# Delta-rule stage of a decoder step: key blocks first, sample work re-placed among the heads' periods

## The reference

```python
decay = jnp.exp(jnp.where(tril, G[..., :, None] - G[..., None, :], -jnp.inf))
kb = k * beta[..., None]
A = jnp.where(tril & (eye == 0), jnp.einsum('bhncd,bhnsd->bhncs', kb, k) * decay, 0.0)
Tm = lax.linalg.triangular_solve(eye + A, jnp.broadcast_to(eye, A.shape), left_side=True, lower=True)
u = Tm @ (v * beta[..., None])
w = Tm @ (kb * jnp.exp(G)[..., None])
...
v_new = u_n - w_n @ S
o = qg_n @ S + qk_n @ v_new
S = S * gl_n[..., None, None] + jnp.swapaxes(kd_n, -1, -2) @ v_new
```

## Time and profile before

| | us |
|---|---|
| median of 3 timed runs | 2983.39 (2982.0 to 2985.71) |
| profiled execution, its own time | 2976.36 |
| its span in the trace | 2974.6 |
| delta-rule stage, barrier to barrier | 1072.3 to 1277.9 |
| TensorE, VectorE, ScalarE, GpSimd busy in the span | 2795.1, 2312.4, 1363.6, 316.1 |

### The profile page before, as it was taken

How to read it: one execution, slowest core, us unless ns; L and a number is a source line. 1 busy time by engine, 2 the same in 40 slices (tenths; PEclk the granted TensorE clock), 3 DMA queues, 4 the chain that set the end, 5 groups by cost and what they waited for, 6 DMA issues and landing times.

```text
span 2974.6 us, 55263 instructions
## 1 busy us (share of the span) xinstructions
PE 2795.1 (94%) x22589; PEld 2669.7 (90%) x22589; DVE 2312.4 (78%) x3566; ACT 1363.6 (46%) x2316; POOL 316.1 (11%) x303
## 2 busy tenths in 40 slices
PE   8999999989988968889889999999999999999995
PEld 8999999988877657789889999999999999999995
DVE  6656777877677778755688888888888888888898
ACT  5434455556545624521254444444444453434352
POOL 0010000024270212323300000000000000000010
PEclk9999999999999989999999999999999999999998
DMA  7564443458632864563343434444443465434333
GB/s 221 177 203 109 128 120 108 120 193 277 227 138 99 358 173 116 147 169 94 90 157 112 140 106 135 123 127 121 121 139 112 138 190 167 146 119 156 103 122 117
DMA packets 520849, 440.12 MB, mean 148 GB/s; under 512 B 36184, under 2 KB 476687, under 8 KB 513979
## 3 DMA queue, kind: packets, MB, share of 16 engines
q1 hardware_dynamic: 456278, 301.49, 35.3%
q0 software_dynamic: 20048, 82.12, 7.4%
q10 hardware_dynamic: 44272, 52.98, 5.3%
HBM read 378.31 MB, written 66.55 MB: 150 GB/s over the span
## 4 chain that ended last, share of the span: by engine, by line
PE 49%; DVE 6%; issue 1%; ACT 1%; DMA 0%; DVEq 0%; ACTq 0%
PE i L3219 42%; PE i L140 7%; DVE f_half L3709 1%; DVE x_blocks L3747 1%; PE i L3207 1%; DVE y_rows L3829 0%; DVE y_rows L3834 0%; DVE h_rows L3742 0%; DVE resid L3594 0%; DVE resid L3597 0%; DVE w_ring L3698 0%; DVE x_blocks L3615 0%; PE i L3228 0%; DMA x_blocks<-s_blk 0%; DVE ln_parts L3753 0%
## 5 line engine op out<-in xcount | busy, mean ns | idle before, releaser
L3219 PE MATMUL i<-x_blocks,f_half 128*128 128x272 f32 x10752 | 1361.1, 289 | 23.4 <-DVE h_rows L3742 11.1
L3219 PEld LDWEIGHTS i<-x_blocks,f_half 128*128 128x128 f32 x10752 | 1351.7, 189 | 28.5 <-DVE x_blocks L3747 12.2
L570 PE MATMUL a<-xb_in,w_half 128*128 128x272 f32 x4200 | 545.5, 291 | 8.2 <-DVE w_half L972 4.2
L570 PEld LDWEIGHTS a<-xb_in,w_half 128*128 128x128 f32 x4200 | 534.9, 189 | 17.2 <-issue 7.2
L3440 ACT CAST f_half<-w_ring 128x1024 fp32r<-128x1024 f32 (+2 forms) x370 | 346.3, 936 | 405.6 <-PE i L3219 351.1
L3709 DVE TENSOR_TENSOR f_half<-w_ring,f_half 128x1024 fp32r<-128x1024 f32 (+2 forms) x362 | 393.0, 1086 | 80.7 <-ACT f_half L3440 78.0
L3709 DVE TENSOR_TENSOR f_half<-f_sum,f_half 128x1024 fp32r<-128x1024 f32 (+2 forms) x148 | 159.4, 1077 | 82.0 <-ACT f_half L3440 82.0
L972 DVE TENSOR_TENSOR w_half<-w_ring,w_half 128x1024 fp32r<-128x1024 f32 x129 | 157.4, 1222 | 79.3 <-ACT w_half L708 78.9
L3440 ACT CAST f_half<-f_sum 128x1024 fp32r<-128x1024 f32 (+2 forms) x148 | 138.7, 937 | 149.7 <-PE i L3219 149.7
L708 ACT CAST w_half<-w_ring 128x1024 fp32r<-128x1024 f32 x125 | 131.3, 1050 | 109.7 <-PE a L570 106.0
L3192 POOL TENSOR_TENSOR f_half<-w_ring,f_half 128x512 fp32r<-128x512 f32 x8 | 13.8, 1731 | 1410.5 <-ACT f_half L3440 1410.5
(11 more groups left out here) (559 smaller groups left out, 4084.3 us busy)
## 6 DMA issues: line engine op xcount, KB each, us to landing
w_ring<-in_ffn_w_up_dram SPq DMA_DIRECT2D x88, 1024.0 KB, 6.0
w_ring<-in_w_in_dram SPq DMA_DIRECT2D x52, 1024.0 KB, 8.8
w_ring<-in_ffn_w_down_dram SPq DMA_DIRECT2D x24, 1536.0 KB, 7.0
w_ring<-in_w_o_dram SPq DMA_DIRECT2D x16, 1024.0 KB, 6.0
x_blocks<-s_blk ACTq DMA_DIRECT2D x17, 816.0 KB, 5.2
s_proj<-st ACTq DMA_DIRECT2D x48, 272.0 KB, 2.6
s_blk<-x_sums ACTq DMA_DIRECT2D x22, 544.0 KB, 6.7
kv_ring<-in_cmp_w_dram SPq DMA_DIRECT2D x16, 512.0 KB, 8.0
```

The costliest lines, as they stand in the source:

```text
L570: last = nc.tensor.matmul(ps[bank][:, 0:HT2], half(q, w)[:, k], XB[v[j]][:, k], start=j in (0, 1, 3) and k == 0 and i == 0, stop=k == HK - ...
L3219: last = nc.tensor.matmul(ps[bank][:, 0:HT2], half(e, j, wl_)[:, s], XB[:, x0 + s, xl_, BLK_OF[j]], start=start and s == 0 and i == 0, sto ...
```

## The change

Opening (period -1). TensorE makes all key blocks first, then head 0's rows, the sample keys, head 0's key products, and the rest. VectorE takes the blocks ahead of the samples' work, which is spread between block rows. ScalarE instead of VectorE scales the sample tiles (8 instructions a tile). The state products and what follows leave the period.

Half of `keys_decayed` now stands behind the third `state_step`, two instructions before the end, and only the second half signals aq_r. The diff, cut to its core:

```diff
 SyncE, rows_in(h)
-                        sp.wait_ge(kk_ps, h - 1)
+                        sp.wait_ge(kk_ps, 2 * (h - 1))
 GpSimd
+                def s_lows(src, dst, at, n):
+                    gp.wait_ge(s_hi, n)
+                    for m, q in enumerate(at):
+                        nc.gpsimd.tensor_tensor(dst[32 * q:32 * q + NS].rearrange("p h d -> p (h d)"), src.rearrange("p h d -> p (h d)"),
+                                                dst[0:NS].bitcast(F32).rearrange("p h d -> p (h d)"), ALU.subtract).then_inc(s_lo, 1)
+                        gp.wait_ge(s_lo, 2 * n - 1 + m)
+
+                def states_decayed(h):
+                    nc.gpsimd.tensor_tensor(SSA[:, h], SSA[:, h], GLS[:, :, h:h + 1].broadcast_to((P, B, HD)), ALU.mult).then_inc(sg, 1)
+
                 for i in PERIODS:
                     lev, new, old, _ = heads(i)
+                    if i == 1:
+                        gp.wait_ge(sg, 3)
+                        s_lows(VNS[:], VN4, (1, 3), 2)
                     if new is not None:
                         if new == 0:
                             gp.wait_ge(x_l, X_DONE + 1)
+                        else:
+                            gp.wait_ge(scaled_r, 2 * new + 1)
...
+                    if i == -1:
+                        gp.wait_ge(tt_i, 2)
+                        s_lows(KDS_F[:], KDS, (2, 3), 1)
+                    if i == 0:
+                        gp.wait_ge(wsp_s, GH // 2)
+                        gp.wait_ge(pre, 1)
                     if old is not None:
-                        gp.wait_ge(wsp_s, 1)
-                        gp.wait_ge(pre, 1)
-                        nc.gpsimd.tensor_tensor(SSA[:, old], SSA[:, old], GLS[:, :, old:old + 1].broadcast_to((P, B, HD)), ALU.mult).then_inc(sg, 1)
-                        gp.wait_ge(s_lo, 2)
...
+                    if 0 <= i <= 2:
+                        for h in range(3 * i, min(3 * i + 3, GH)):
+                            states_decayed(h)
 TensorE
-                def keys(h):
+                def keys(h, k):
                     r = h % 2
-                    pe.wait_ge(nat_r, h + 1)
-                    pe.wait_ge(scaled_r, 2 * h + 2)
-                    for t in range(QT):
+                    if k == 0:
+                        pe.wait_ge(nat_r, h + 1)
+                        pe.wait_ge(scaled_r, 2 * h + 2)
+                    for u in range(2):
+                        t = 2 * k + u
...
-                def s_states():
+                def s_states(h2):
...
                     if i == -1:
+                        key_blocks(0, GH).then_inc(kx_ps, 1)
+                        rows(0)
                         s_keys()
-                        key_blocks(0, 6)
                         s_turn()
-                        rows(0)
+                        keys(0, 0)
+                        keys(0, 1)
                         s_y()
-                        key_blocks(6, GH).then_inc(kx_ps, 1)
+                        s_values()
                         s_d()
-                        s_values()
-                        keys(0)
                         pe.wait_ge(inv_s, 1)
                         s_w()
-                        s_states()
                         continue
...
                     if done is not None:
                         step_s(done, 3)
+                        sample_s(done, 1)
                     if i == 0:
+                        s_states(0)
+                    if i == 1:
                         s_o()
                     if lev is not None:
                         products_d(lev, 4)
+                    if i == 0:
+                        s_states(2)
...
 ScalarE
+                def s_scaled(dst, c):
+                    for h in range(GH):
+                        last = nc.scalar.mul(dst[:, h], ps[6 + h // 4][0:NS, (h % 4) * HD:(h % 4 + 1) * HD], c[:, h:h + 1])
+                    return last
...
+                    if i == 1:
+                        act.wait_ge(vn_s, 1)
+                        s_highs(VNS[:], VN4, (0, 2))
...
-                    if i == 0:
-                        s_squares()
...
+                    if i == 1:
+                        s_squares()
 VectorE, opening
-                s_decay()
                 blocks_log()
+                s_decay()
                 scaled_keys(0)
-                s_keys()
                 decay(0)
-                dve.wait_ge(k_ps_s, 1)
-                s_scaled(((KGS, BE[0:NS, QC]), (KDS_F[:], ED[0:NS, QC]))).then_inc(k_r_s, 1)
-                s_turned()
+                blocks_weights()
                 scaled_queries(0)
-                blocks_weights()
                 blocks_keys()
...
-                dve.wait_ge(vp_s, 1)
-                s_rows(VNS, 0).then_inc(vn_s, 1)
 VectorE, one period
                     if new is not None:
                         scaled_keys(new)
+                    if done is not None:
+                        sample_states(done, 1)
                     if lev is not None:
                         place_d(lev, 4)
-                    if i == 0:
+                    if i == 1:
                         dve.wait_ge(op_s, 1)
                         s_rows(ONS, 1).then_inc(or_s, 1)
...
+                    if new is not None:
+                        keys_decayed(new, 0)
                     if old is not None:
                         state_step(old, 1)
+                        sample_states(old, 0)
                     if i == 0:
-                        s_lows(KDS_F[:], KDS, (2, 3), 1)
-                        s_lows(VNS[:], VN4, (1, 3), 2)
-                        s_normed()
-                    if new is not None:
-                        keys_decayed(new)
-                    if old is not None:
-                        sample_states(old, 0)
-                        v_copy(old, 2)
+                        keys_decayed(new, 1)
...
+                    if i == 2:
+                        s_normed()
                     if old is not None:
+                        v_copy(old, 2)
...
                         state_step(old, 2)
-                        sample_states(old, 1)
+                        if new is not None:
+                            keys_decayed(new, 1)
                         v_copy(old, 3)
```

105 lines of the change are left out of this document (56 added, 49 removed).

## The result

The changed kernel takes 2967.66 us (median of 6 runs, 2961.14 to 2973.05), the kernel before 2984.5 us on the same chip (also 6 runs). The ratio is 0.9946, 95% interval 0.9935 to 0.9958. The change was measured against the kernel before in two more sets of runs, further down: 0.996 (0.9949 to 0.9972) and 0.9965 (0.9951 to 0.9978). The mean of the three is 0.9957, some 13 us.

The account below looks back on a forecast made before the run. Hand-overs between engines were taken to bound the stage, no engine or memory being full. Terms 3.2 + 3.0 + 0.3 - 1.0 + 6.0 - 0.3 = 11.2 us off the median 2983.39 gave 2972.2 us, range 2963.5 to 2980.5.

Parts of the forecast that it names:

- Opening: Delta-rule stage before head 0's first level product: scaling groups and waits leave VectorE's queue, 3.2 us off (2.0 to 4.8).
- Period 0: Head 0's period: VectorE work leaves, state products fill TensorE's idle time, clock mostly full; 3.0 us off (1 to 4.5).
- Period 1: Head 1's period: sample copies on VectorE, s_o on TensorE, low halves on GpSimd; 0.3 us off (-1.5 to 2).
- Period 2: Head 2's period: two decays meet the query scaling, sample norm and s_out add time; 1.0 us on (-1 to 3).
- Periods 3 to 6: Decay product gone, GpSimd waits for VectorE's scaled keys: 1.5 us off each, 6.0 in all (0 to 8).
- (a): Periods 3 to 6: TensorE's wait of 0.59 at L2313 goes, the w copy is next late; 0.7 us.
- (b): Periods 3 to 6: half the key products moved, so L2281 starts once VectorE's level-5 placement is done; another 0.7 us.
- (c): Periods 3 to 6: behind step v 2 the second key half replaces the second sample state product; 0.1 us in all.
- Tail: Stage end: the last head's second state addition stands before its norm, about half already on the path; 0.3 us on.
- The slowing moves but stays: Rival: GpSimd's work meets other two-input VectorE work, periods 3 to 6 stay at 18.5 us; 2978.2 us, chance 0.17.
- The opening gives little: Rival, with period 0: s_placed waits, clock stays half; 2.0 and 1.0 us for 3.2 and 3.0; 2975.4 us, chance 0.12.
- The late half of the keys: Slower case: each head's first level product waits for VectorE's second decayed half; at 3 us late 2993.2 us, chance 0.07.

Follow-up runs that it names:

- after_again2: The changed kernel, unchanged, run and profiled again in the first follow-up set: 2980.92 us, ratio 0.9960 to the kernel before.
- after_again3: The changed kernel, unchanged, run and profiled again in a later set: 2972.93 us, ratio 0.9965 to the kernel before.
- p2_wait2: The changed kernel with the last two decays waiting until VectorE has scaled head 3's queries: 2973.26 us, ratio 0.9935 to the kernel before.
- lows_late_p2: The changed kernel with the last two decays behind head 3's scaled queries and GpSimd's sample-key low halves behind head 1's: ratio 0.9940 to the kernel before.
- before_wait: The kernel before with one line added, GpSimd's spreads wait for the scaled keys: ratio 0.9994 to the kernel before.
- scaled_on_dve: The changed kernel with the samples' scaling back on VectorE: ratio 0.9975 to the kernel before.
- decay_each2: The changed kernel with one decay a period ahead of the masked values, spreads still waiting for scaled keys: ratio 0.9977 to the kernel before.
- keys_whole: The changed kernel with TensorE's four key products in one piece ahead of the level-6 Y products: ratio 0.9971 to the kernel before.

## Why the forecast held, and where it did not

The predicted time, 2972.2 us, is 4.5 above the measured 2967.66, and the predicted gain of 11.2 us lies between the 10.6 and 16.8 us of the three comparisons. But the parts did not all come out, and their misses cancelled for the greater part: in the first pair period 0, period 2 and the tail gave 5.7 us less than forecast, and the opening, period 1 and periods 3 to 6 gave 3.5 more. Here is the stage by its steps, the changed kernel's three profiles against two or three of the old stage.

**Opening, 3.2 off expected (2.0 to 4.8); 5.2 in the first pair and 4.4 in the second, 2.8 to 6.1 if all profiles are paired.** The mechanism is right: VectorE's queue is the path, and the groups are 3.6 us. The step at issue was whether s_placed waits for s_d. In the first profile it did not: L2830 starts at 1088.06 right behind the decayed keys, since head 0's key products ran at full clock (1.99 us). In after_again2 they did too, but VectorE waited 1.49 us for the sample keys before that, and the opening was 30.1. In after_again3 s_placed waited 1.62 us, behind key products of 3.44 us, at a clock of 0.61 for the stretch, and the opening was 30.9:

```profile
1096.71 0.43 DVE L2830 COPY_PREDICATED inv_t_s<-kv_ring,g 32x256 f32<-32x256 int32 x1 [1.62 <-PE g L2416]
```

So both ends that the forecast left open occur, from one execution to the next, and they go with TensorE's clock. In the first pair the good end is better than thought by 0.4.

**Period 0, 3.0 off expected (1 to 4.5); 1.4 in the first pair and 3.9 in the second, 21.3 to 22.1 us against 23.5 and 25.2.** The old kernel's own clock in the period was 0.78 and 0.71, which makes most of the difference between the pairs. The mis-sized term is the clock's recovery. The forecast charged 0.9 us for the first product group; that group did take 2.08, but the first 16 state products (32 instructions) behind it also took 3.68 (first profile) or 2.96 for 1.97, another 1.0 to 1.7 us (2.96 is p2_wait2's):

```profile
1097.74 2.08 PE L2303 MATMUL g<-t_inv,kv_ring 128*128 128x128 f32 x8 [4.91 <-POOL t_inv L2230]
1099.74 3.68 PE L2442 MATMUL g<-kv_ring,mix 128*64 128x128 f32 x32
```

Behind them the period ran at full clock almost without gaps, as the forecast had it. VectorE's slowing beside the low halves (6.23 us for 1.13) was not seen coming, and lows_late_p2 shows that it cost nothing.

**Period 1, 0.3 off expected (-1.5 to 2); 1.25 off.** Within its bounds. The low halves do cross the query products (1.23 and 1.41 us for 0.69 each), the masked values are 0.31 late. What the step left out: period 1 has the same pair of slowed key products as its successors. before_wait gains 1.4 us in this period with the wait alone.

**Period 2, 1.0 on expected (-1 to 3); 4.7 on, 4.5 to 5.7 in the three profiles.** This is the step that failed. It named the collision (two decays meet the query scaling) and priced it at 1.5 us. The collision itself is 2.8 us, since both query products are hit, 1.90 and 2.28, where the earlier trace rows had one product at 2.29. And it stopped there: it did not ask what TensorE's waiting would do to the clock, although period 0 of the kernel before showed the half clock behind waits. The half clock adds another 2.2 us in the first profile (23.2 against scaled_on_dve's 21.0). p2_wait2 takes the collision away and the period falls to 18.2, which is 0.3 off instead of 1.0 on. The sample norm and output cost 1.3 us (18.21 against 16.88 in p2_wait2's next period) where 1.05 was summed: that term was about right.

**Periods 3 to 6, 1.5 off each expected; 1.65.** Here every step can be checked, since the experiments form a chain: 18.50, with the wait alone 17.77, with the key products split and the state product moved 17.31 to 17.36 (decay_each2), with the decays away 16.85. Step (a), 0.7: 0.73. Steps (b) and (c), 0.7 and 0.1: 0.44 together, and keys_whole has 0.42 for the split alone; step (b) was over-sized, because the moved half (0.87) finds only 0.33 us of idleness behind step v 2. The last 0.47 was in no step: with the decay gone from each period, the masked values end before the query scaling begins, which took 1.15 us for its first product in decay_each2 (there TensorE then waits 0.22 us for VectorE's level-5 placement, here it does not). The reasons for the sum were thus two-thirds right, and the third that was missing made up for the step that was too large. The wait at L2313 is gone and no w copy took its place in the timeline; TensorE's waits left in period 4 are these two:

```profile
1184.88 0.66 PE L2389 MATMUL g<-consts,o_rows 128*128 128x128 f32 x4 [0.30 <-DVE o_rows L2791]
...
1193.79 0.49 PE L2363 MATMUL g<-kv_ring,inv_t 128*128 128x128 f32 x2 [0.22 <-DVE state L2778]
```

**Tail, 0.3 on expected; 0.7 on** in the first pair, 0.6 in the second. The direction is right. The forecast took half of the 0.68 us as covered; that none of it was is a reading of these two differences, and no run tests it.

**The rivals.** "The slowing moves but stays" was placed in periods 3 to 6 and happened in period 2 instead, with a larger price. "The opening gives little" did not occur in any profile; "period 0 gives little" did in part. The late half of the keys, the slower case, is excluded: in periods 3 to 6 no wait stands before the next head's first product. The condition was real, though: in period 0, where VectorE's second half stands late, TensorE waits 0.34 us for it.

**The rule of the Trainium skill** on the interfaces that GpSimd shares with VectorE ("GPSIMD Engine Reference", sections 1 and 8) carried the forecast and holds in every experiment here, in the rows with two SBUF inputs and in the PSUM-fed ones that stayed at 0.43. The traces add that what matters is not how much GpSimd does but what VectorE begins at that time, and that the price is the rest of GpSimd's instruction (the 0.55 us above).

**Sum.** The forecast's 11.2 us for the stage stand against 9.0 and 10.6 in the two pairs of profiles. The medians of the three comparisons differ by 16.8, 10.8 and 10.6 us. In the first profiled pair 5.4 us lay ahead of the stage, where the changed kernel's execution had the higher clock, so the larger first difference is not shown to be the change's. That the forecast came within 4.5 us is in part luck: its parts missed both ways.
